# Expert layer in blocks of 32 rows instead of 64, on four column tiles of TensorE instead of two

## What is computed

```python
g_logits = xt @ w_group + b_group            # 4 groups
e_logits = xt @ w_router + b_router          # 8 experts in each group
grp = argmax(g_logits); top_v, top_i = top_k(e_logits[grp], 2)
gate_w = softmax(top_v) * p_grp              # two experts for each token
for e, toks in blocks_of_tokens_sorted_by_expert:
    xb  = xt[toks]                                          # rows of 1024
    hid = silu(xb @ w_e_gate[e]) * (xb @ w_e_up[e])         # 512 wide
    y[toks] += gate_w * (hid @ w_e_down[e])
x = x + gt2 * y;  out = rmsnorm(x, g_final)
```

## Time and profile before

| what | value |
|---|---|
| median of 3 runs | 1874.75 us (1870.53 to 1879.89) |
| the profiled execution's own time | 1872.36 us |
| its span, first to last instruction | 1870.0 us |
| PE busy | 1672.3 us (89%) |
| DVE busy | 974.8 us (52%) |
| ACT busy | 493.4 us (26%) |
| POOL busy | 193.3 us (10%) |
| DMA, mean over the span | 169 GB/s |
| expert stage, from the first L1207 to the end of the last L1225 | 1210.8 to 1837.8 us |

### The profile page before, as it was taken

The page is one execution under the profiler, slowest core; times in us unless marked ns, Lnnn a source line. Parts: engine busy times, 40 slices in busy tenths (PEclk is TensorE's granted clock), DMA queues, the critical chain, the costliest instruction groups (busy, mean ns, idle before and its releaser), DMA issues.

```text
span 1870.0 us, 22711 instructions
## 1 busy us (share of the span) xinstructions
PE 1672.3 (89%) x7893; PEld 865.2 (46%) x7894; DVE 974.8 (52%) x1920; ACT 493.4 (26%) x976; POOL 193.3 (10%) x369
## 2 busy tenths in 40 slices
PE   1897879999999898999999999399999989999882
PEld 0663354655654555667667455233333333333331
DVE  6567767877878667455655433433333323333223
ACT  2115334544543657010010111011111111111112
POOL 0010000000000000000000000112222222222120
PEclk9898989999999999999999999599999999999996
DMA  8562101010000111111211812789999846999995
GB/s 281 187 218 86 57 23 30 28 46 12 1 1 1 57 29 40 34 34 34 67 34 45 329 68 94 283 316 398 394 321 397 308 135 218 398 401 363 401 398 205
DMA packets 111096, 316.62 MB, mean 169 GB/s; under 512 B 15080, under 2 KB 52968, under 8 KB 86448
## 3 DMA queue, kind: packets, MB, share of 16 engines
q1 hardware_dynamic: 99280, 287.88, 40.5%
q0 software_dynamic: 11744, 27.79, 6.1%
HBM read 289.14 MB, written 26.51 MB: 169 GB/s over the span
## 4 chain that ended last, share of the span: by engine, by line
PE 78%; DVE 9%; DMA 6%; ACT 4%; issue 2%; SPq 1%; DVEq 0%; POOLq 0%; ACTq 0%; POOL 0%
PE ps L1207 18%; PE ps L1147 9%; PE ps L1225 9%; PE ps L1136 6%; PE ps L1161 6%; PE ps L1008 5%; PE ps L1033 4%; PE ps L1058 4%; DMA arena<-in_w_e_up_dram 3%; PE ps L1014 3%; PE ps L1084 3%; PE ps L962 3%; PE ps L1044 2%; ACT arena L792 2%; DVE arena L1392 2%
## 5 line engine op out<-in xcount | busy, mean ns | idle before, releaser
L1207 PE MATMUL ps<-arena 128*64 128x512 f32 x1632 | 379.0, 607 | 18.7 <-DMA arena<-in_w_e_up_dram 10.9
L1736 DVE COPY arena<-ps 128x256 f32<-128x256 f32 x51 | 21.7, 425 | 396.1 <-ACT arena L893 396.1
L1207 PEld LDWEIGHTS ps<-arena 128*64 128x64 f32 x1632 | 115.7, 139 | 235.4 <-issue 228.2
L1225 PE MATMUL ps<-arena 128*64 128x512 f32 x816 | 186.3, 598 | 0.5 <-ACT arena L897 0.5
L1147 PE MATMUL ps<-rounded 128*128 128x512 f32 x768 | 183.3, 398 | 0.0
L1410 DVE TENSOR_SCALAR_CACHE_REDUCE arena<-arena,small 128x384 bf16<-128x384 f32 (+2 forms) x204 | 181.5, 940 | 0.0
L1147 PEld LDWEIGHTS ps<-rounded 128*128 128x128 f32 x768 | 144.2, 188 | 36.6 <-issue 7.6
L695 POOL DMA_INDIRECT sum_rows<-arena,ones x51 | 81.4, 1595 | 439.3 <-DVE arena L1758 420.1
L1008 PE MATMUL ps<-arena 128*128 128x512 f32 x256 | 116.8, 610 | 4.8 <-ACT arena L758 3.4
L1473 DVE CUSTOM_DVE_ANT_0 arena<-ps,arena 128x896 f32<-128x896 f32 (+7 forms) x128 | 91.7, 754 | 53.5 <-PE ps L1033 53.2
L1058 PE MATMUL ps<-arena 128*64 128x128 f32 x1152 | 96.4, 286 | 23.3 <-ACT arena L792 21.8
(11 more groups left out here) (265 smaller groups left out, 1906.8 us busy)
## 6 DMA issues: line engine op xcount, KB each, us to landing
arena<-in_w_e_gate_dram SPq DMA_DIRECT2D x32, 2048.0 KB, 15.0
arena<-in_w_e_up_dram SPq DMA_DIRECT2D x32, 2048.0 KB, 20.7
arena<-in_w_e_down_dram SPq DMA_DIRECT2D x32, 2048.0 KB, 15.7
arena<-in_w_mod_dram SPq DMA_DIRECT2D x12, 2048.0 KB, 8.6
arena<-in_w_in_dram SPq DMA_DIRECT2D x33, 512.0 KB, 4.3
arena<-in_x_dram SPq DMA_DIRECT2D x16, 512.0 KB, 12.4
sum_rows<-arena SPq DMA_DIRECT2D x9, 512.0 KB, 2.6
arena<-cum_rows SPq DMA_DIRECT2D x8, 512.0 KB, 5.1
```

The lines of the kernel that those rows point to most:

```text
L1207: m = pe.matmul(ps[o * TB:(o + 1) * TB, 2, 0:2 * FQ].rearrange("p (j n) -> p j n", j=2), xT[:, k % NX, k // NX * TB:(k // NX + 1) * TB], w ...
L1225: m = pe.matmul(ps[o * TB:(o + 1) * TB, 5, 0:DQ], hidT[:, k % NH_T, k // NH_T * TB:(k // NH_T + 1) * TB], w_dn[c][:, k, o * DQ:(o + 1) * D ...
```

## The change

The block has 32 rows on four column tiles (NT = 4): BLOCKS becomes 96, AHEAD 8, ROWS 104. A block is then 128 partitions by 256 columns; a gate/up matmul has 256 columns instead of 512, a down matmul 256 instead of 512, and there are four of them for each slice instead of two. RUN, the most blocks that one expert can have, becomes 32. The weights are laid out so that each partition gets one run of 16 KB for gate and one for up; for that the columns of the input rows are written in another order, and the columns of gate and up are read with a step of two. The sums are kept in two tensors, one for even and one for odd blocks; the second is filled with zeros early, and both are added at the end. A scatter no longer waits for the one just before it. The code of an expert has two copies of `token_block`: one for the first block, one in three nested loops.

```diff
-NT = 2
+NT = 4
-    y_d = nc.dram_tensor("sum_rows", (S + P, D), F32).ap()
+    y_d = [nc.dram_tensor(f"sum_rows{z}", (S + P, D), F32).ap() for z in range(2)]
...
+            sp.wait_ge(win_ok, 1)
+            for k in range(2):
+                sp.dma_start(y_d[1].rearrange("(t q) (k n) -> q t k n", q=P, k=2)[:, :, k, :],
+                             zeros.unsqueeze(1).to_broadcast([P, TT + 1, 512])).then_inc(zero_out, 16)
...
-                    sp.dma_start(w_gu[c][:, j].rearrange("p (q t) n -> p q t n", q=NT),
-                                 w[0, ORDER[e]:ORDER[e] + 1].rearrange("o (q p t) n -> p (o q) t n", q=NT, p=P)).then_inc(wgu_in[c], 16)
+                    sp.dma_start(w_gu[c][:, j],
+                                 w[0, ORDER[e]].rearrange("(p t) n -> p t n", p=P)).then_inc(wgu_in[c], 16)
...
             for t in range(TT):
-                sp.dma_start(x1[:, t, :], y_d[t * P:(t + 1) * P, :]).then_inc(x_in[t], 16)
+                sp.dma_start(x1[:, t, :], y_d[0][t * P:(t + 1) * P, :]).then_inc(x_in[t], 16)
+                sp.dma_start(yb[:, t, :], y_d[1][t * P:(t + 1) * P, :]).then_inc(x_in[t], 16)
...
                         pool.wait_ge(ye_ok, b + 2)
                         pool.wait_ge(idxs_ok, b + 1)
-                        pool.wait_ge(y_out[1 - z], 8 * AHEAD * i + 16 * ((q + 1) // 2))
                         pool.sem_inc(stand, 1)
-                        pool.indirect_dma_start(y_q, bass.IndirectOffsetOnAxis(idx_s[q][:, 0:1], 0), ye[z], None, compute_op=ALU.add).then_inc(y_out[z], 16)
+                        pool.indirect_dma_start(y_q[z], bass.IndirectOffsetOnAxis(idx_s[q][:, 0:1], 0), ye[z], None, compute_op=ALU.add).then_inc(y_out[z], 16)
...
-                rows_t = xrow.rearrange("r (p t) -> r t p", t=NX)
+                rows_t = xrow.rearrange("r (t p) -> r t p", t=NX)
...
-                                      xT[:, k % NX, k // NX * TB:(k // NX + 1) * TB], w_gu[c][:, :, k, o * FQ:(o + 1) * FQ],
+                                      xT[:, k % NX, k // NX * TB:(k // NX + 1) * TB], w_gu[c].rearrange("p j k (q n t) -> p j k q t n", q=2, t=2)[:, :, k, o // 2, o % 2, :],
...
                 with pe.If(1 < blocks):
-                    token_block(first + 1, c, own)
-                with pe.If(2 < blocks):
-                    token_block(first + 2, c, own)
-                with pe.If(3 < blocks):
-                    with pe.Fori(3, RUN) as k:
-                        with pe.If(k < blocks):
-                            token_block(first + k, c, own)
+                    with pe.Fori(0, RUN // 16) as k0:
+                        with pe.If(16 * k0 + 1 < blocks):
+                            with pe.Fori(0, 4) as k1:
+                                with pe.If(16 * k0 + 4 * k1 + 1 < blocks):
+                                    with pe.Fori(0, 4) as k2:
+                                        with pe.If(16 * k0 + 4 * k1 + k2 + 1 < blocks):
+                                            token_block(first + (16 * k0 + 4 * k1 + k2 + 1), c, own)
...
             def modulate_a2():
                 dve.wait_ge(mbc_ok, 8)
+                dve.tensor_copy(sh2.rearrange("q (k p) -> q p k", k=KT), sh2_p.rearrange("q (p k) -> q p k", k=KT)).then_inc(mbc_ok, 1)
...
-                link(dve.scalar_tensor_tensor(h2[t % 2], x1[:, t, :], rstd[:, t:t + 1], a2, ALU.mult, ALU.mult))
+                link(dve.scalar_tensor_tensor(h2[t % 2].rearrange("q (k p) -> q p k", k=KT), x1[:, t, :].rearrange("q (p k) -> q p k", k=KT),
+                                              rstd[:, t:t + 1], a2.rearrange("q (p k) -> q p k", k=KT), ALU.mult, ALU.mult))
...
+            def both(t):
+                dve.wait_ge(x_in[t], 64)
+                dve.tensor_tensor(x1[:, t, :], x1[:, t, :], yb[:, t, :], ALU.add).then_inc(x1_ok, 1)
+
+            both(0)
             for t in range(TT):
+                if t + 1 < TT:
+                    both(t + 1)
```

More of the change, by code:

```diff
@@ L126, in build @@
     h2_d = nc.dram_tensor("h2_rows", (S, D), F32).ap()
-    y_d = nc.dram_tensor("sum_rows", (S + P, D), F32).ap()
+    y_d = [nc.dram_tensor(f"sum_rows{z}", (S + P, D), F32).ap() for z in range(2)]
     h2_q = h2_d.rearrange("s (q d) -> (s q) d", q=NT)
-    y_q = y_d.rearrange("s (q d) -> (s q) d", q=NT)
+    y_q = [y.rearrange("s (q d) -> (s q) d", q=NT) for y in y_d]
     cum_d = nc.dram_tensor("cum_rows", (NH, S), F32).ap()
@@ L226, in build @@
         pT_a = [at(u, 512) for u in (36, 36.5, 14, 14.5)]
+        zeros = at(15, 512)
         oT = [[at(u, U) for u in (25, 27, 28, 29)], [at(37 + p, U) for p in range(PAIRS)]]
@@ L240, in build @@
         gt1, sh2, a2, gt2 = acc[2:6]
+        sh2_p = at(13, U)
         wO = [[at(8 + 3 * z, U, [KT, P]), at(9 + 3 * z, U, [KT, P]), at(10 + 3 * z, 512, [4, P]), at(10.5 + 3 * z, 512, [4, P])]
@@ L306, in build @@
         idx_s = [ones[:, 48 + 2 * q:50 + 2 * q].bitcast(I32) for q in range(AHEAD)]
+        yb = at(8, 8 * U, [TT, D])
         gfin = acc[2]
@@ L338, in build @@
         x1_out = sem("x1_out")
+        zero_out = sem("zero_out")
         g_sub = sem("g_sub")
@@ L627, in _ @@
             pool.wait_ge(ip_ps, TT)
+            pool.memset(zeros, 0.0).then_inc(win_ok, 1)
             link(pool.memset(sc[:, 0:MOFF[B0]], 0.0))
@@ L677, in _ @@
             pool.wait_ge(x1_out, 16 * (TT + 1))
+            pool.wait_ge(zero_out, 32)
             with pool.Fori(0, BLOCKS // AHEAD) as i:
@@ L806, in high @@
                 if kt == 0:
+                    act.wait_ge(zero_out, 32)
                     act.wait_ge(lg_done, 2 * (N_B + TT))
@@ L921, in _ @@
             for t in range(TT):
-                act.wait_ge(x_in[t], 48)
+                act.wait_ge(x1_ok, 2 * TT + t + 1)
                 if t >= 1:
@@ L1122, in _ @@
                     values(n, groups - 1)
-            pe.wait_ge(mbc_ok, 9)
+            pe.wait_ge(mbc_ok, 10)
             pe.wait_ge(o_done, N_U)
@@ L1492, in out_a @@
                 dve.tensor_copy(oT[0][p][:, b * P:(b + 1) * P], ps[:, 6, 0:P]).then_inc(o_done, 1)
-            dve.wait_ge(win_ok, B0)
+            dve.wait_ge(win_ok, 1 + B0)
             def signs_back():
@@ L1535, in modulate @@
                 dve.wait_ge(mbc_ps, n + 1)
-                dve.tensor_tensor(acc[2 + n // 2][:, half], ps[:, 7, :], bmb[:, n // 2, half], ALU.add).then_inc(mbc_ok, 1)
+                dve.tensor_tensor((sh2_p if n // 2 == 1 else acc[2 + n // 2])[:, half], ps[:, 7, :], bmb[:, n // 2, half], ALU.add).then_inc(mbc_ok, 1)
             def modulate_a2():
                 dve.wait_ge(mbc_ok, 8)
+                dve.tensor_copy(sh2.rearrange("q (k p) -> q p k", k=KT), sh2_p.rearrange("q (p k) -> q p k", k=KT)).then_inc(mbc_ok, 1)
                 dve.scalar_tensor_tensor(a2, a2, 1.0, gffn, ALU.add, ALU.mult).then_inc(mbc_ok, 1)
```

14 lines of the change are left out of this document (7 added, 7 removed).

## The result

The changed kernel takes 1906.45 us (median of 4 runs, 1905.5 to 1907.93), the kernel before 1875.64 in the same comparison (4 runs, 1870.53 to 1879.89). The ratio is 1.0168, interval 1.015 to 1.0186: slower by 1.7%. The forecast was 1925 with a range of 1850 to 1975.

The account below looks back on a forecast made before the run. The prediction took TensorE to bound the expert stage, with the weights touching the bound. Its terms, -106 + 112 + 7 + 26 - 2 + 9 + 7 = +53 on 1872.4 us, gave 1925 us, range 1850 to 1975.

Parts of the forecast that it names:

- The work of the blocks: TensorE in the expert stage: 79 blocks of 6.22 us, 491 us, replace 598 us of larger blocks; -106 us.
- The loops: PE's sequencer: 85 skipped rounds at 0.85 us, loop exits and uncovered expert changes leave PE idle; +112 us.
- the lead is some 16 records: PE's sequencer runs some 16 records ahead, so down's last 16 records cover 0.9 us of loop control.
- Between blocks: Within one expert, a loop path of some 1.05 us against 0.9 of cover, 47 blocks x 0.15; +7 us.
- The clock: PE restarts at a slower clock after idle gaps; 14 gaps over 5 us at 2.0 each, less today's one; +26.
- Weights: PE's waits for the weight stream: two short ones, 9 us against 10.9; long runs worth nothing; -2 us.
- The two sums and the tail: At the end, doubled loads and a full-width addition per tile cost some 9.5 us, last scatters return 0.5; +9.
- Without it the -106 would be gone: Scatters in the expert stage: without the removed wait between them, a 6.22 us beat could not hold, losing the -106.
- Dispatch and the rest: Larger dispatch table, second norm's scaling, the shift's copy and POOL's clearing of zeros; together +7 us.
- the skips are covered: Rival, chance 0.15: longer sequencer lead or cheap false conditions remove loop and clock costs; weights end last, 1829 to 1840 us.
- The scatters hold the beat: Rival, chance 0.06: scatter landings behind longer runs stretch the block beat to 6.7 up to 9 us; 1950 to 2055 us.
- Four tiles don't run abreast: Rival, chance 0.07: TensorE runs only two column tiles at a time, about 2300 us; a milder form gives 2030.

Follow-up runs that it names:

- The kernel with the dynamic end: Changed kernel with its three nested loops replaced by one loop from 1 to the expert's own number of blocks: 1841.91 us, ratio 0.9829 to the kernel before.
- the loops of before: Changed kernel with copies for the second and third block and one loop from 3 to the longest run, a condition each round, replacing the nested loops: 2188.12 us.

## Why the prediction was right

The time lies in the range, on the side given 0.7, and 19 us below the forecast of 1925. On the footing of the sum (spans), +53 was forecast and +36.2 came. Step by step:

- **The work of the blocks, -106.** The beat is 6.25 to 6.27 us without a new middle round where 6.22 was worked out, so 79 x 6.26 - 51 x 11.72 = -103. Four tiles run abreast as two do. Gate/up, which reads its columns with the step of two, is a little slower than down, which does not. Their matmuls, both of 256 columns, by the lines (min/median/max):

```profile
L1218 PE MATMUL ps<-arena x5056: 385/388/637, 1216.5 to 1859.9; 128*32 128x256 f32 x195
L1236 PE MATMUL ps<-arena x2528: 376/379/403, 1227.7 to 1864.9; 128*32 128x256 f32 x195
```

From one four of matmuls to the next it is 0.227 us in gate/up and 0.216 in down, so the 16 steps of a block take 0.18 us more, 14 us in 79 blocks, where 0 was taken and up to 1.7 a block bounded. No run separates the step from the longer pattern that it is part of, so whether a step of two is free, as the prediction read it, stays open. The beat came out right all the same, by luck, because the two turns took 0.63 us (1253.26 to 1253.52, 1255.46 to 1255.83) where 0.77 were put in: 16 x 0.227 + 8 x 0.216 + 0.63 is 5.99, and 0.27 is left for restarts.
- **The loops, +112.** "issue" rose by 94.5 (100.7 against 6.2). The price of a skip was right (0.74 to 0.86 in the trace, 0.83 by doubling the middle loop; 0.85 was taken), and so were the counts. The term that was mis-sized is the cover: "the lead is some 16 records", so that down covers 0.9 us. At the ends of the halves and of down in the changed kernel's stage 20 matmuls are left when the sequencer moves on, which with the last one's length is 1.45 us of cover. 31 x 0.55 is 17 us, the whole difference; that it fits so well is luck, since smaller misses cancel. A change of expert took 2.0 to 2.5 us of the sequencer where 2.0 was put in, and the first pass through the code of the loop has two gaps of 2.25 and 4.37 us for which there was no term; the skips and exits took some 75 us where 82 were put in. The two rows of before bounded it badly: there 14 of 16 matmuls were left, because down has no more than 16 and two start together. The Trainium skill ("TensorE: Matmul & The Clock Gate", Architectural detail) has a depth of 64; by the prediction's reading of it all of down would have been cover. The trace says 20 matmuls with 16 or 17 loads, neither the one nor the other.
- **Between blocks, +7.** +3, for the same reason: the longer cover holds the path of the inner loop. Only where a middle round begins, 19 times, does gate/up start 0.16 us later.
- **The clock, +26.** 17 blocks restart at half clock, 35.5 us above their undisturbed length; before it were 3 with 6.5. That is +29. 15 of the 17 stand behind an expert with more than one block, where the prediction counted 14.
- **Weights, -2.** 5.3 against 10.9, -5.6. That long runs are worth nothing was right.
- **The two sums and the tail, +9.** +8.7. "Without it the -106 would be gone" was too strong beside the nested loops (+36), and nearly right without them (+64.5).
- **Dispatch and the rest, +7.** +5.7: the table matmuls took 11.26 us instead of 8.05, two products 3.69 instead of 2.50.

The measured terms, with "issue" for the loops, sum to -103 + 94.5 + 29 - 5.6 + 8.7 + 5.7 = +29; 7 us of the 36.2 are left. They are busy time of PE in the stage, since its busy time fell by 66.5 where the two terms on blocks and clock say 74, and idle time can't show them. Without a stop gate/up starts 1.75 us after down did (1255.83 to 1257.58), before down's 1.93 are over; at each of the 30 stops that overlap of 0.18 is lost, 5 us, and the 3 between blocks come on top, less 1 in the kernel before.

So the mechanism was as forecast, and the misses are of size. The forecast is 17 too high in spans: 17.5 for the loops, 4 each between blocks and for the weights and 2 in the small terms, less 3 each for the beat and the clock and 5 for the overlap, which had no term.

Of the rivals, *the skips are covered* gave 1829 to 1840 with some 65 us of waits for weights. The kernel with the dynamic end is in effect that case: 1841.9, with 49 us of waits. *The scatters hold the beat* did not come: with two sums no wait of PE for them is in the profile. *Four tiles don't run abreast* fell with the beat.

What the prediction did not weigh is why the change has its two copies and three loops. Of the loops of before it says only that "today one expert in 32 pays it"; around blocks of 32 rows they take 2188 us.

## What to carry to other kernels

A round of a hardware loop that only tests and goes on costs the sequencer some 0.8 us, and it is hidden only by what the engine has queued, here 20 matmuls, 1.45 us; count skips as instructions, and where the number of rounds is in a register, let the loop end there. Smaller blocks pay only where loops, length of code and chained scatters are cheap beside the shorter beat; what ends last then (here the weights) sets what is left of the gain. An added wait is not priced by a run in which a gap stands beside it: the same wait cost 36 us with the nested loops and 64.5 without them.

## What the runs showed of the hardware

- PE's code has a size at which branches become dear: with 2376 instructions in the loop over experts 48 branches took 211 us, up to 8.3 each, and 115 packets of code were fetched in the stage; with 1188 it was one branch of 1.93 us and 8 packets.
- The sequencer's lead over PE is very even: 20 matmuls left at four tiles with 256 columns, 14 at two tiles with 512.
- The interval from scatter to scatter in a chain depends on the stream beside it: 9.7 to 11.9 us while weights come in, 4.6 to 4.8 when none do.
- VectorE's operations with two full-width inputs, started during a GpSimd addition, took 2.75 to 3.28 us instead of 1.14 to 1.28.
- Half clock after a gap costs the same after 6.25 and after 9.53 us of idle time (3.64 us for the first half of gate/up instead of 2.02, granted clock 0.50).
- Where gate/up starts without a stop it overlaps with down by 0.18 us; each stop loses that beside its idle time, and shows it as busy time.
